# A float32 mixer, feed-forward, deltanet and band-attention chain on one core: joined column tiles in the down projections, x turned later, neighbourhood scores as split products

## What is computed

```python
h = rms_norm(x, norm_mix)
uv, qkv, gates = split(h @ w_in)                    # w_in: 2048 x 9216
y_a = u * (w_s @ layer_norm(v) + b_s)               # gMLP branch, u, v = gelu(uv)
s = q @ k.T * scale + bias[rpb]                     # 16 heads of 64, neighbourhood window
y_b = softmax(s) @ v
x = x + (sigmoid(g_a) * (y_a @ w_branch[:1024]) + sigmoid(g_b) * (y_b @ w_branch[1024:])) @ w_out

up = conv3(rms_norm(x, norm_ffn) @ w_up)            # w_up: 2048 x 11008, taps over the rows
x = x + (silu(gate) * val) @ w_down                 # w_down: 5504 x 2048
x = rms_norm(x, norm_final)
...                                                 # second block: gated deltanet, band attention
```

## Time and profile before

| | |
|---|---|
| median of 3 runs | 2291.66 us (2291.44 to 2291.88) |
| the profiled execution | 2291.97 us, span 2290.2 us |
| busy in the span | PE 2283.1, DVE 1462.8, ACT 1342.2, POOL 70.3 us |
| weight loads on PE | 1887.1 us, beside its matmuls |
| granted clock of TensorE, mean | 1.0 |
| DMA | 510.61 MB, mean 223 GB/s |

### The profile page before, as it was taken

How to read it: one execution, slowest core, us unless ns; L and a number is a source line. 1 busy time by engine, 2 the same in 40 slices (tenths; PEclk the granted TensorE clock), 3 DMA queues, 4 the chain that set the end, 5 groups by cost and what they waited for, 6 DMA issues and landing times.

```text
span 2290.2 us, 29601 instructions
## 1 busy us (share of the span) xinstructions
PE 2283.1 (100%) x11199; PEld 1887.1 (82%) x11199; DVE 1462.8 (64%) x2019; ACT 1342.2 (59%) x1974; POOL 70.3 (3%) x94
## 2 busy tenths in 40 slices
PE   9999999999999999999999999999999999999999
PEld 7887778888888888888888888888888888888887
DVE  5757555556666665466766677787977665555554
ACT  5557564444566564365665576667674556566653
POOL 0011100000200000000000001010000000000000
PEclk9999999999999999999999999999999999999999
DMA  8789996667888876588886756675755788977974
GB/s 269 219 264 264 262 247 219 215 214 216 255 246 237 241 230 200 178 253 236 246 235 196 241 158 199 172 212 164 228 157 177 223 258 228 259 223 227 265 223 164
DMA packets 463678, 510.61 MB, mean 223 GB/s; under 512 B 188305, under 2 KB 284337, under 8 KB 463409
## 3 DMA queue, kind: packets, MB, share of 16 engines
q1 hardware_dynamic: 457408, 500.30, 74.4%
q10 hardware_dynamic: 6128, 8.43, 1.1%
HBM read 428.94 MB, written 45.89 MB: 207 GB/s over the span
## 4 chain that ended last, share of the span: by engine, by line
PE 95%; DVE 2%; ACT 1%; DVEq 1%; DMA 0%; issue 0%; ACTq 0%
PE gemm L777 30%; PE gemm L778 29%; PE gemm L779 29%; DVE w_lo L748 1%; PE aux L779 1%; PE aux L778 1%; PE aux L777 1%; PE aux L2450 1%; ACT w_hi L738 1%; PE aux L2859 0%; PE aux L2845 0%; PE aux L2640 0%; PE aux L2528 0%; PE aux L2545 0%; PE aux L2652 0%
## 5 line engine op out<-in xcount | busy, mean ns | idle before, releaser
L748 DVE TENSOR_TENSOR w_lo<-raw,w_hi 128x1024 fp32r<-128x1024 f32 (+1 forms) x800 | 953.2, 1205 | 552.9 <-ACT w_hi L738 548.4
L738 ACT ACTIVATE w_hi<-raw 128x1024 fp32r<-128x1024 f32 (+1 forms) x800 | 817.5, 1039 | 485.2 <-PE gemm L779 341.8
L777 PE MATMUL gemm<-w_lo,hT 128*128 128x512 f32 x2304 | 903.0, 392 | 1.5 <-DVE hT L1651 0.9
L779 PE MATMUL gemm<-w_hi,hT 128*128 128x512 f32 x2304 | 893.8, 388 | 0.0
L778 PE MATMUL gemm<-w_hi,hT 128*128 128x512 f32 x2304 | 893.7, 388 | 0.0
L777 PEld LDWEIGHTS gemm<-w_lo,hT 128*128 128x128 f32 x2304 | 432.8, 188 | 95.1 <-issue 4.7
L779 PEld LDWEIGHTS gemm<-w_hi,hT 128*128 128x128 f32 x2304 | 432.6, 188 | 89.6
L778 PEld LDWEIGHTS gemm<-w_hi,hT 128*128 128x128 f32 x2304 | 432.9, 188 | 85.6 <-issue 0.2
L777 PE MATMUL gemm<-w_lo,yT_hi 128*128 128x512 f32 x472 | 184.3, 391 | 0.1
L779 PE MATMUL gemm<-w_hi,yT_lo 128*128 128x512 f32 x472 | 183.7, 389 | 0.0
L778 PE MATMUL gemm<-w_hi,yT_hi 128*128 128x512 f32 x472 | 183.6, 389 | 0.0
(11 more groups left out here) (347 smaller groups left out, 1804.1 us busy)
## 6 DMA issues: line engine op xcount, KB each, us to landing
raw<-in_w_up SPq DMA_DIRECT2D x336, 256.0 KB, 3.7
raw<-in_w_in SPq DMA_DIRECT2D x144, 512.0 KB, 4.9
raw<-in_a_w_in SPq DMA_DIRECT2D x128, 512.0 KB, 4.1
raw<-in_b_w_in SPq DMA_DIRECT2D x128, 512.0 KB, 4.5
raw<-in_w_down SPq DMA_DIRECT2D x76, 512.0 KB, 4.5
raw<-in_w_branch SPq DMA_DIRECT2D x32, 512.0 KB, 5.2
raw<-in_w_out SPq DMA_DIRECT2D x32, 512.0 KB, 4.4
raw<-in_a_w_out SPq DMA_DIRECT2D x32, 512.0 KB, 4.4
```

Of the source, the lines that this page charges most:

```text
L738: nc.scalar.activation(hi, src, ACT.Copy).then_inc(S("hi_done"), 1)
L748: nc.vector.tensor_tensor(lo, src, hi.bitcast(F32), ALU.subtract).then_inc(S("lo_done"), 1)
L777: nc.tensor.matmul(dst, xh, wl[:, k, :], start=h["start"] and k == 0, stop=False)
L779: mm = nc.tensor.matmul(dst, xl, wh[:, k, :], start=False, stop=h["stop"] and k == h["n"] - 1)
```

## The change

It has five parts.

- **Scores in parts.** q and k are split like weights (`hi_of_rows` on ACT, `lo_of_rows` on DVE, into memory that is free at that time), and a group of scores is 24 float32r matmuls in place of 8 float32 ones. PE waits for the low parts instead of the turns. The second turn of k goes out one load earlier.
- **Joined column tiles.** The plan takes the first two column tiles of each down projection together: all loads of the first but the last, the same of the second, then the last load (two halves) of the one and of the other. The other two tiles stay as they were.
- **The last up tile by DMA.** It goes the way of the others: words apart on ACT, plane write before half 7 of the first column tile, turn at half 1 of the second. `turn_last` and its copies out of PSUM go.
- **The turns of x.** All three lie in the third and fourth column tile now: planes are written before halves 3 and 11 of the third and before half 6 of the fourth; the turns stand at half 5 of the third and at halves 1 and 8 of the fourth, the last two behind a new wait for DVE to be done with the stage (`stage_free`).
- **Bias copies and constants.** The skewed bias copies become sixteen DMAs of one head, one in three halves. `wsT` and `bsT` are loaded in the middle of the fourth tile of `w_in` with a semaphore of their own, `wsT` is split last, and the mixing's semaphores are merged into one for each engine.

```diff
--- before.py
+++ after.py
     parts = [(t, *p, True, True) for t, p in enumerate(parts)]
+    for t, loads in downs[::-1]:
+        parts[t:t + 2] = ([(t + j, loads[:-1], "y", 0, 512, True, False) for j in range(2)]
+                          + [(t + j, loads[-1:], "y", sum(loads[:-1]), 512, False, True) for j in range(2)])
...
+            def down_tiles(loads, k0, j0, tiles, third={}, fourth={}):
+
+                first, second = up_turn(j0, tiles - 2), up_turn(j0, tiles - 1, 7, 1)
+                first["before"] = {**first["before"], **second.pop("before")}
+                for i in range(2):
+                    tile("down", loads[:-1], i * 512, k0, **(second if i else first))
+                for i in range(2):
+                    tile("down", loads[-1:], i * 512, k0 + sum(loads[:-1]))
+                tile("down", loads, 2 * 512, k0, **third)
+                tile("down", loads, 3 * 512, k0, **fourth)
...
-                sp.wait_ge(S(f"na_copied{u // 2}"), 16)
+                sp.wait_ge(S(f"na_copied{u // 2}"), 4 * 16)
...
-                for i in range(4):
-                    tile("down", DOWN2, i * 512, 2 * UP1, **(turn_rows(X_TURNS[2] + i - 1, 8) if i else up_turn(UP1, UP2 - 2)))
+                x_turns = [turn_rows(X_TURNS[2] + j, at) for j, at in enumerate((3, 11, 6))]
+
+                def stage_free(j, ready):
+
+                    sp.wait_ge(S("hT_lo_done"), 8 * 2 + 2 * j)
+                    ready()
+                third = dict(before={**x_turns[0]["before"], **x_turns[1]["before"]},
+                             ready=x_turns[0]["ready"], behind=x_turns[0]["behind"])
+                fourth = dict(before=x_turns[2]["before"],
+                              ready={1: lambda: stage_free(1, x_turns[1]["ready"][13]), 8: lambda: stage_free(2, x_turns[2]["ready"][8])},
+                              behind={1: x_turns[1]["behind"][13], **x_turns[2]["behind"]})
+                down_tiles(DOWN2, 2 * UP1, UP1, UP2, third, fourth)
...
+            def hi_of_rows(n, dst, src):
+                act.wait_ge(S("qk_turned"), 32 * (n + 1))
+                A(dst[:, :, :], src[:, :, :], ACT.Copy).then_inc(S("qk_hi"), 1)
...
+            def bias_copies():
+                for h in range(NAH):
+                    copy_bias(na_skew, ins["na_rpb"], SKEW, f"na_copied{h // 4}", h, 1)
+                    yield
+                    yield
+                    yield
...
-                if last:
-                    act.wait_ge(S("up_last_turned"), j0 // UP1 + 1)
-                    act.wait_ge(S("conv_val_done"), n - 1)
-                    for b in range(2):
-                        A(sums[:, 2 * b:2 * b + 2, :], AX[b][:, :].rearrange("p (a t) -> p a t", a=2), ACT.Copy)
-                    act.drain()
...
+            def lo_of_rows(n, dst, src, hi):
+                dve.wait_ge(S("qk_hi"), n + 1)
+                V.tensor_tensor(dst[:, :, :], src[:, :, :], hi[:, :, :].bitcast(F32), ALU.subtract).then_inc(S("qk_lo"), 1)
...
                     if n % 2 == 0:
-                        pe.wait_ge(S("qk_turned"), 32 * (2 + n))
+                        pe.wait_ge(S("qk_lo"), 2 + n)
...
                         for tb in range(TB):
-                            for a in range(2):
-                                rows_ = slice(a * NAD, (a + 1) * NAD)
-                                m = MM(score_banks(u % 2)[a][:, tb * T:(tb + 1) * T], qT[rows_, u % 4, tb * P:(tb + 1) * P],
-                                       kT[rows_, u % 4, :], start=True, stop=True)
-                                if tb:
-                                    m.then_inc(S("na_scores"), 1)
+                            for part, (q_part, k_part) in enumerate(((qT_lo, kT_hi), (qT_hi, kT_lo), (qT_hi, kT_hi))):
+                                for a in range(2):
+                                    rows_ = slice(a * NAD, (a + 1) * NAD)
+                                    m = MM(score_banks(u % 2)[a][:, tb * T:(tb + 1) * T], q_part[rows_, u % 4, tb * P:(tb + 1) * P],
+                                           k_part[rows_, u % 4, :], start=part == 0, stop=part == 2)
+                                    if tb and part == 2:
+                                        m.then_inc(S("na_scores"), 1)
...
-                turn_rows(up_rows, (0, 1), "up_last_turned")
...
-                run(half, 2 * len(loads) - 4, turn_last(t0 + tiles - 1))
+                run(half, 2 * len(loads) - 4)
                 pe.wait_ge(S("act_lo"), j0 + tiles - 2)
                 run(half, 2)
+                run(half, 2 * len(loads) - 2)
                 pe.wait_ge(S("act_lo"), j0 + tiles - 1)
                 half()
                 pe.wait_ge(S("act_lo"), j0 + tiles)
                 half()
-                for s in range(3):
+                run(half, 2)
+                for s in range(2):
                     run(half, 2 * len(loads))
```

More of the change, by code:

```diff
@@ L557, in _ @@
             tile("in", FOUR, 0)
-            for j in range(4):
-                tile("in", [4], 512, 4 * j)
+            tile("in", [4, 4], 512)
+            sp.dma_start(wsT[:, :, :], ins["gm_w_s"]).then_inc(S("mix_landed"), 16)
+            sp.dma_start(bsT[:, :], ins["gm_b_s"]).then_inc(S("mix_landed"), 16)
+            tile("in", [4, 4], 512, 8)
             for g in range(2):
@@ L1003, in turn_x, with down_x @@
                     yield
-            def down_x(s, t):
-                yield
+            def down_x(s, t, behind):
+                for _ in range(behind + 1):
+                    yield
                 x_apart(2, s, t)
@@ L1104, in attend @@
                 for step in range(55):
+                    if step == 26:
+                        hi_of_rows(2, qT_hi, qT)
+                    for n, at in enumerate((0, 28)):
+                        if step == at:
+                            hi_of_rows(2 * n + 1, kT_hi, kT)
                     for n, at in enumerate((1, 10, 29, 37)):
@@ L1121, in attend @@
                     yield
-            mix = mixing()
+            def bias_copies():
+                for h in range(NAH):
+                    copy_bias(na_skew, ins["na_rpb"], SKEW, f"na_copied{h // 4}", h, 1)
+                    yield
+                    yield
+                    yield
+            mix, copies = mixing(), bias_copies()
             for t in range(4):
-                run(half, 8 if t else 0, mix if t >= 2 else none)
+                run(half, 8 if t else 0, mix if t >= 2 else none, copies)
                 tile_done(act, pl, t)
@@ L1136, in _ @@
                     t = 4 + 3 * g + part
-                    run(half, 8, mix, side, att if g else none)
+                    run(half, 8, mix, side, att if g else none, copies)
                     finish(side)
@@ L1685, in out_x, with down_x @@
                     yield
-            def down_x(s):
+            def down_x(s, behind):
+                for _ in range(behind):
+                    yield
                 dve.drain()
@@ L1844, in _ @@
                     t = 4 + 3 * g + part
-                    run(half, 8, mix, att if g else none)
+                    run(half, 8, mix, att if g else first_lo() if part == 2 else none)
                     tile_done(dve, pl, t)
@@ L1913, in _, with up_side @@
                 add_tile(T_OUT + s, s * 512)
-            def up_side(j0, n, last=False):
+            def up_side(j0, n):
                 blk0, kt, w = up_blocks(j0, n)
+                last = n == (UP2 if j0 else UP1) - 1
                 n = j0 + n
                 gate, val, sums = cg[n % 2], cv[n % 2], ut[n % 2]
-                for _ in range(4 if last else 2):
+                for _ in range(5 if last else 2):
                     yield
@@ L1960, in feed_forward @@
                     up_read(t0 + n, j0, n)
-                run(half, 2 * len(loads) - 1, up_side(j0, tiles - 2), up_side(j0, tiles - 1, True))
+                run(half, 2 * len(loads) - 3, up_side(j0, tiles - 2))
+                run(half, 2 * len(loads) - 2, up_side(j0, tiles - 1))
+                run(half, 2)
+                turns = [down_x(s, 6 if s == 1 else 0) if j0 else none for s in range(3)]
                 add_tile(t_down, 0)
-                for s in range(1, 4):
-                    run(half, 2 * len(loads), down_x(s - 1) if j0 else none)
-                    add_tile(t_down + s, s * 512)
+                run(half, 2, turns[0])
+                add_tile(t_down + 1, 512)
+                run(half, 2 * len(loads), turns[0], turns[1])
+                add_tile(t_down + 2, 1024)
+                run(half, 2 * len(loads), turns[1], turns[2])
+                add_tile(t_down + 3, 1536)
             if parts >= 2:
```

108 lines of the change are left out of this document (60 added, 48 removed).

## The result

The changed kernel takes 2296.54 us, the median of 12 runs (2294.91 to 2300.93), against 2291.62 for the kernel before (12 runs, 2291.44 to 2292.62): 1.0023 of it, with a 95% interval of 1.0015 to 1.0031. It is slower by about 0.2%, just over what can be told from no change, and its runs are spread five times as wide. The profiled execution took 2297.43 us, with a span of 2295.4. The 2.0 us around the span are 0.3 more than before; no run here shows why.

A forecast was written before the change was run, and what follows sets the result against it. PE was taken to bound the kernel; -2.4 (scores) - 1.8 (up turns) - 0.2 (joined pair's stop) + 4.6 (x turns) = +0.2 us on the profiled 2291.97 gave 2292.2, or 2291.8 on the runs' scale; range 2286.9 to 2297.4.

The forecast's parts named there:

- the likeliest case: Whole kernel: no change that counts, 2288.5 to 2294.5 us, chance 0.38.
- rival three: Score groups: the two row halves of the array take turns, +2.7 us instead of -2.4, 2296.9 us; chance 0.1.
- rival two: Third column tile, second down projection: plane writes take 7.0 us, delay runs through later turns, 11 lost, 2298.2; chance 0.15.
- What bounds the kernel: Whole kernel: PE, busy 2283.1 of 2290.2 us; time comes only from matmuls dropped or made cheaper and PE's few stalls.
- Last up tile: Both down projections: eight turns leave PE in each, 0.88 us each, 1.8 saved; 0.2 more at the second's joined pair.
- The added SP wait: Before half 7 of the first column tile: load ready at 14.3 us, PE there at 15.0; zero cost, bound 1.
- The x turns, in SP's order: Third and fourth column tiles, second down projection: PE waits 0.3, 1.2, 1.6 and 1.5 us at halves 6, 2, 8, 9; 4.6 lost.
- Scores in parts: Four score groups: 24 float32r matmuls each save 0.6 us a group, 2.4 in all; k's subtraction costs zero.
- I take 1.5: One score group: 12 steps of 0.117 us make 1.40, bound 1.6 with entry and exit; 1.5 taken against 2.13 now.
- Bias copies: ACT: sixteen issues of some 0.63 us for four, 7.6 more, under ACT's lead of two halves; zero cost.

## Why the prediction was right and where it was wrong

The range held the result and the likeliest case did not: I forecast no change that counts, and the kernel is slower by 4.9 us; a time above 2296.2 had a chance of 0.2. That the range held is in part luck, for its upper end covers rival three and the milder part of rival two, and neither happened. Point by point:

- **What bounds the kernel** was right: what moved in the ledger is waits of PE, with their stops, and matmuls that PE no longer does.
- **Last up tile.** The turns were priced right: the first projection is 0.86 us shorter, 0.88 predicted, and in the second the stop of 0.2 at the pair's last load went too. The added SP wait was put at zero, bound 1: it cost 0.74 and a stop. The words were done 7.7 us after the tile's start (7.1 in the sum) and the load took 5.17 (4.5), so the half was ready at 15.7 in place of 14.3, and PE was there at 14.95 as worked out. The margin of 0.7 was smaller than the errors of its terms. With the write before half 9 (above, all planes moved) the wait is gone.
- **The x turns, in SP's order,** were the right step with the right mechanism, and mis-sized by little: 5.47 us of waits in place of 4.6, and stops of 0.12 that the sum left out. In the three other profiles with the same order the waits of these two tiles came to 4.1, 4.8 and 6.0, so the 4.6 lies within what varies. (The sum has a slip of 0.3: 40.6 + 0.9 + 0.9 is 42.4, not 42.7.) The halves named were 6, 2, 8 and 9; the waits came at 6, 8 and 9, with 1.81 and 1.37 for 1.6 and 1.5. Half 6 of the third tile got 2.06 in place of 0.3, because the turn held SP for 5.58 in place of 3.8, over the 5.2 of the earlier trace rows, and the load behind it took 4.98. Half 2 of the fourth got nothing in place of 1.2: the write took 3.0 and the turn 2.8 (4.5 and 4.2 in the sum). Rival two, long writes, was not what happened: the first write landed in 3.11.
- **Scores in parts** failed, in two steps. "I take 1.5" had the 12 steps right (0.117 each) but took too little for the way in and out: a group costs 1.82, so 0.31 is saved and not 0.6. And what the groups save was counted as gained, while PE gives most of it (1.2 us for four groups) back at the next half that needs DVE. I had asked whether k would be ready, which it was (no wait before the third group), and not what follows the scores.
- **Bias copies,** "zero", was wrong: undoing them gave 0.94 us in one pair of profiles, and 0.62 in the other, both counted behind 100 us. Not ACT's issues cost this, which I had priced, but a bias that lands earlier: it puts POOL's masks beside DVE's work.

So the two terms that were to pay for the turns, -2.4 and -1.8, came to -0.2 (the bias copies in it) and -1.7, and of the -1.7 the late half of the last up tile took 0.9 back, so that little stood against the loss.

## What to carry to other kernels

On a queue that works in order, put a wait where its data is already there: holds of 4 to 5 us cost nothing by themselves here, nor 4 behind a wait of 7, but a hold of 5.6 behind a wait of 9 cost 2. A place with 0.2 us of margin costs something in one execution and nothing in the next. When a matmul group feeds a chain on other engines that PE meets again, the time between is the chain's, and a cheaper group buys only what its first result comes earlier. And a transfer that lands sooner can start work on another engine at a worse moment: look at what it triggers, as much as at what it costs.

## What the hardware showed that I had not expected

DVE slows while POOL works: four scalings of 256 columns took 1.14 us with POOL idle and 1.85 or 2.39 beside its selects, a subtraction of 1024 columns up to 1.75 in place of 1.22, and POOL's selects stretched from 0.74 to 1.61. The biased scores, which read PSUM, kept their 0.69: that at 260.56, shown above, ran beside this select and the next:

```profile
259.98 0.73 POOL L876 TENSOR_SCALAR_AFFINE_SELECT bias<-bias 64x576 f32<-64x576 f32 x1
```

The Trainium skill ("SBUF — State Buffer", "Who interferes with whom") has the rule: POOL shares its ports with DVE's second pair, which scalings can use and operations with two inputs in SBUF do; the traces agree with it.

The hold of a turn on SP's queue is not a constant: the fifteen turns of x in the changed kernel and in the four versions with turns moved took 2.81 to 5.88 us. What sets it stays open. It fits with this that the changed kernel's runs spread over 6.0 us, and those of the version with all planes moved, in which PE waits for no turn, over 1.6. But the three slowest of the changed kernel's runs are among the four with a granted clock below 1.0, and no profile of them was kept, so what makes the spread is not shown; without those four runs it is 2.5.
